# First layer's gate modulation on VectorE instead of TensorE, and two more PSUM banks in the second layer

## The chip, the core and the metric

The kernel runs on one NeuronCore of a Trainium2 chip, with float32 inputs and outputs. The metric is the device time of one execution in microseconds (us). TensorE, VectorE, ScalarE, GpSimd and SyncE are called by these names in the text, and PE, DVE, ACT, POOL and SP in the rows of the profile.

## What is computed

Three transformer layers follow each other on 256 tokens, the first also on 256 context tokens: a differential attention layer, a grouped attention layer, and a third with sparse attention, retention and a feed-forward part. The change concerns the modulation of the first two. Each layer multiplies silu(c) and silu(c_ctx) with a matrix `ada_w[i]` of 1024 x 3072. The first third of its product shifts the normed input, the second scales it and the last gates the layer's output.

```python
# first block, layer 0 (differential attention) and layer 1 (grouped attention), over x (256 tokens)
# and ctx (256 tokens), D = 1024
def adaln(cvec, w, b):
    m = jax.nn.silu(cvec) @ w + b
    return jnp.split(m, 3, axis=-1)
...
    for i in range(DEPTH):
        last = i == DEPTH - 1
        shift, scale, gate = adaln(c, ada_w[i], ada_b[i])
        shift, scale, gate = shift[:, None, :], scale[:, None, :], gate[:, None, :]
        cshift, cscale, cgate = adaln(c_ctx, ada_w[i], ada_b[i])
        h = rms_norm(x, pre_g[i]) * (1.0 + scale) + shift
        hc = rms_norm(xc, pre_g[i]) * (1.0 + cscale) + cshift
...
        x = x + gate * rms_norm(y, post_g[i])
        if not last:
            xc = xc + cgate * rms_norm(yc, post_g[i])
    return x
```

## The kernel before

**Products.** All weights stream from HBM in halves of 128 x 4 x 512 numbers (1 MB; "half 0" holds rows 0 to 511 of the matrix, "half 1" rows 512 to 1023) through six buffers `raw`, in the order of `loads_plan`. SyncE issues one load after the other, and load n waits until load n-6 has been used up. ScalarE rounds a half into one of three `w_hi` buffers (line 1372), VectorE writes the rest into `w_lo` (line 1951), and TensorE multiplies in three products for each block of 128 rows (lines 825 to 827). A unit (stage, c, t) is one column chunk c of 512 columns for one tile t of 128 tokens, 8 blocks and so 24 products.

**Modulation products.** `ada_half` (line 847) does without the split: four products of 32 rows each with `cstat`, straight from `raw`. `BESIDE_IN0` says beside which unit of the first layer's input stage `in0` such a pair of halves is worked off. Before the change the gate's two chunks ("ada0g", 0) and ("ada0g", 1) stand beside units (0, 3) and (1, 1), and the four chunks of the second layer's shift and scale ("ada1", 0 to 3) beside (2, 1), (3, 1), (4, 1) and (5, 0). ScalarE copies the product out of PSUM (`move`, line 1454). For shift and scale `mod_columns` (line 861) then turns the rows into columns, beside the units of `COLUMNS_IN0`, and VectorE adds the bias (`mod_sums`, line 2103). For the gate `gate_row` (line 871) multiplies the rows with `sel`, which spreads them to all partitions.

**The stage in0.** Units (0, 0) to (5, 3) run in this order on TensorE. Chunks 0 to 3 are queries and keys, and after unit n TensorE turns unit n-2 (line 922). ScalarE handles each unit in the order: copy of the turned unit n-2 (line 1505), then the copy of a modulation product of the unit before, then for chunks 4 and 5 the copy of the values. VectorE takes at tile 0 of chunk c the split of the half that comes third from the chunk's start. After unit (5, 2) TensorE computes the first two score blocks, then unit (5, 3), and then it waits for the first probabilities: 32 steps of attention (p = 0 to 31) with the units of chunks 6 and 7 between them. For them VectorE runs, in this order, `max0(0)`, `max0(1)` (line 2199), `comb0(0)`, `comb0(1)` (lines 2208 to 2214), the split of half 1 of chunk 6, and `max0(2)`. `comb0(p)` releases TensorE's turn of the probabilities (line 928). The exponentials between them are ScalarE's (line 1529).

**The stage in1.** Here the second layer's units (c, t) run. TensorE turns the context tiles' features in pairs of two blocks, `norm1c`, half of them after unit (2, 0), the other half after unit (2, 1) (`NORM_IN1`, line 885). A pair fills one PSUM bank, which VectorE frees once it has written the rests of both blocks (`lo1`, lines 2355 and 1986). Before the change pairs 0 and 1 use banks 4 and 5, and pairs 2 and 3 use them again. Unit (2, 2) is the first that reads these features, and it waits for the rest of each block. `GATE_IN1` places the second layer's gate rows after units (1, 0) and (2, 1), and VectorE finishes them in `gates1` (lines 2288 and 2291) in the unit after. When the units are done, TensorE waits until all turned blocks have been copied, and starts the second layer's scores.

## Times and profile before

| | us |
|---|---|
| three runs, median (lowest, highest) | 799.34 (798.61, 799.36) |
| the profiled execution | 799.71 |
| its span | 797.6 |

The profile shows one execution. The span is what lies between its first and last instruction, and 2.1 us of the execution's own time lie around it. A row of a timeline gives start, duration, engine, source line, operation, output and inputs, how many were merged into the row, and in brackets the idle time of the engine before it and what ended it.

### The profile page before, as it was taken

The numbers are of one execution on the slowest core, as the hardware profiler recorded it, in microseconds if no ns is written. First come the engines' busy times: TensorE is split into PE (matmuls) and PEld (weight loads), VectorE is DVE, ScalarE is ACT, GpSimd is POOL, SyncE is SP. The second block draws the span as 40 slices with busy tenths as digits, with TensorE's granted clock in tenths as the row PEclk, the third lists the DMA queues.
The fourth block names the chain that finished last, engine by engine and source line by source line (L and its number), as shares of the span: only waits on it lengthen the run. The fifth ranks groups of instructions, "written<-read, shape, count | busy, mean of one in ns | idle before, by whom it ended". The sixth has DMA issues, their size and how long they took to land.

```text
span 797.6 us, 11013 instructions
## 1 busy us (share of the span) xinstructions
PE 786.0 (99%) x4108; PEld 625.5 (78%) x4108; DVE 503.7 (63%) x873; ACT 394.0 (49%) x728; POOL 42.9 (5%) x55
## 2 busy tenths in 40 slices
PE   8999999999999999999999999999999999999998
PEld 5577787778777777777778887887788888888886
DVE  3475445225767875779856678799887645455454
ACT  3541313235878773575647646735345433443431
POOL 0120000000001001101100001300000000000000
PEclk9999999999999999999999999999999999999999
DMA  9974542464100046338333026983216665566521
GB/s 337 387 243 159 211 161 83 178 211 160 52 1 1 1 151 246 106 106 310 139 106 106 2 65 211 334 298 106 80 54 211 211 202 167 161 210 210 181 84 53
DMA packets 71303, 125.56 MB, mean 157 GB/s; under 512 B 2714, under 2 KB 28652, under 8 KB 71124
## 3 DMA queue, kind: packets, MB, share of 16 engines
q1 hardware_dynamic: 70208, 122.47, 44.2%
q0 software_dynamic: 512, 1.18, 0.6%
q10 hardware_dynamic: 532, 1.21, 0.4%
q8 instruction: 33, 0.54, 0.3%
q14 instruction: 18, 0.15, 0.1%
HBM read 123.79 MB, written 1.06 MB: 157 GB/s over the span
## 4 chain that ended last, share of the span: by engine, by line
PE 86%; DVE 6%; ACT 3%; DMA 2%; issue 1%; POOL 1%; SPq 1%; DVEq 0%; ACTq 0%
PE psum L825 20%; PE psum L827 19%; PE psum L826 19%; PE psum L1005 3%; PE psum L1335 3%; PE psum L928 3%; PE psum L1333 3%; PE psum L1334 3%; PE psum L1034 2%; PE psum L847 2%; DMA act_lo_as_f<-in_ada_w 2%; PE psum L1107 2%; DVE w_lo L1951 2%; PE psum L922 1%; PE psum L914 1%
## 5 line engine op out<-in xcount | busy, mean ns | idle before, releaser
L826 PE MATMUL psum<-w_lo,act_hi 128*128 128x512 f32 (+1 forms) x752 | 291.8, 388 | 0.0
L825 PE MATMUL psum<-w_hi,act_hi 128*128 128x512 f32 (+1 forms) x712 | 289.5, 407 | 1.2 <-DVE act_lo L2355 0.7
L827 PE MATMUL psum<-w_hi,act_lo 128*128 128x512 f32 (+1 forms) x712 | 276.9, 389 | 0.0
L1951 DVE TENSOR_TENSOR w_lo<-raw,w_hi 128x2048 fp32r<-128x2048 f32 (+1 forms) x70 | 157.9, 2263 | 104.9 <-ACT w_hi L1372 104.8
L1372 ACT ACTIVATE w_hi<-raw 128x2048 fp32r<-128x2048 f32 (+1 forms) x74 | 140.1, 1897 | 72.4 <-PE psum L827 36.9
L825 PEld LDWEIGHTS psum<-w_hi,act_hi 128*128 128x128 f32 x712 | 133.7, 188 | 43.6 <-issue 17.6
L826 PEld LDWEIGHTS psum<-w_lo,act_hi 128*128 128x128 f32 x752 | 141.6, 188 | 25.3 <-issue 1.0
L827 PEld LDWEIGHTS psum<-w_hi,act_lo 128*128 128x128 f32 x712 | 133.6, 188 | 28.6
L1919 POOL TENSOR_TENSOR rstd<-ms,half_neg 128x1 f32<-128x1 f32 (+3 forms) x38 | 36.3, 957 | 551.4 <-DVE ms L1992 551.4
L1529 ACT ACTIVATE sc<-psum,nmax 128x512 f32<-128x512 f32 (+1 forms) x64 | 36.9, 589 | 20.5 <-DVE nmax L2199 20.5
L1454 ACT ACTIVATE sc<-psum 128x512 f32<-128x512 f32 (+1 forms) x62 | 32.6, 527 | 15.3 <-PE psum L928 8.5
L2199 DVE TENSOR_REDUCE nmax<-psum 128x2 f32<-128x1024 f32 (+1 forms) x32 | 30.5, 954 | 10.3 <-PE psum L1005 10.2
L1334 PE MATMUL psum<-w_lo,act_hi 128*128 128x512 f32 x88 | 34.2, 389 | 0.0
L1875 ACT ACTIVATE sc<-psum 128x256 f32<-128x256 f32 x22 | 8.5, 385 | 50.5 <-PE psum L827 50.5
L1333 PE MATMUL psum<-w_hi,act_hi 128*128 128x512 f32 x80 | 31.2, 390 | 0.0
L1335 PE MATMUL psum<-w_hi,act_lo 128*128 128x512 f32 x80 | 31.1, 389 | 0.0
L928 PE MATMUL psum<-ident,sc 128*128 128x128 f32 x184 | 29.6, 274 | 1.0 <-ACT sc L1830 0.9
L1034 PEld LDWEIGHTS psum<-vbuf,sc 128*128 128x128 f32 x192 | 26.2, 191 | 3.6 <-ACT sc L1454 1.0
L1034 PE MATMUL psum<-vbuf,sc 128*128 128x128 f32 x192 | 26.7, 275 | 0.4 <-ACT sc L1454 0.4
L2785 DVE SCALAR_TENSOR_TENSOR sc<-sc,psum 128x256 f32<-128x256 f32 x22 | 9.2, 419 | 23.9 <-ACT sc L1875 23.9
L928 PEld LDWEIGHTS psum<-ident,sc 128*128 128x128 f32 x184 | 21.7, 142 | 2.5 <-ACT sc L1830 1.7
L1505 ACT ACTIVATE round_k<-psum 128x512 fp32r<-128x512 f32 x8 | 4.8, 599 | 33.6 <-PE psum L922 33.6
(272 smaller groups left out, 991.2 us busy)
## 6 DMA issues: line engine op xcount, KB each, us to landing
raw<-in_a_w_in SPq DMA_DIRECT2D x16, 1024.0 KB, 9.6
raw<-in_ada_w SPq DMA_DIRECT2D x16, 1024.0 KB, 5.3
raw<-in_w_out SPq DMA_DIRECT2D x12, 1024.0 KB, 5.2
raw<-in_w_gate SPq DMA_DIRECT2D x22, 512.0 KB, 4.2
raw<-in_w_up SPq DMA_DIRECT2D x22, 512.0 KB, 5.2
raw<-in_w_down SPq DMA_DIRECT2D x11, 1024.0 KB, 4.9
raw<-in_b_w_in SPq DMA_DIRECT2D x10, 1024.0 KB, 7.3
raw<-in_w_in SPq DMA_DIRECT2D x10, 1024.0 KB, 6.0
```

The costliest lines, as they stand in the source:

```text
L825: pe.matmul(oh, x_hi, hi, start=(k == 0), stop=False)
L826: pe.matmul(o[:, 0:n], x_hi, lo, start=False, stop=False)
L827: mm = pe.matmul(oh, x_lo, hi, start=False, stop=(k == KT - 1))
L928: mm = pe.transpose(o[:, tile_cols(i)], src[:, tile_cols(i)], ident[:])
L1034: mm = pe.matmul(o[:, 0:P], probs[:, tile_cols(i)], vbuf[:, NT - blocks + i, tile_cols(h)], start=(i == 0), stop=(i == blocks - 1))
L1333: pe.matmul(oh, x_hi, hi, start=(j == 0 and i == 0), stop=False)
L1334: pe.matmul(o, x_hi, lo, start=False, stop=False)
L1335: mm = pe.matmul(oh, x_lo, hi, start=False, stop=(last and i == 1))
L1372: ins = act.activation(hi, weights, ACTF.Copy)
L1529: seq.freed(act.activation(sc[:, 2 * (p % 2) + s, 0:n], psum[:, b, 0:n], ACTF.Exp, bias=nmax[:, p % 2, s:s + 1], accum_out=rsum[:, p % 2, ...
L1919: seq.note(pool.tensor_tensor(rstd[:, n:n + w], ms[:, n:n + w], half_neg[:, 0:w], ALU.pow).then_inc(s_powout, 1), s_powout)
L1951: ins = dve.tensor_tensor(rest, weights, hi.bitcast(F32), ALU.subtract)
```

## The change

The gate's product of the first layer is no longer taken on TensorE. VectorE multiplies each block of weight rows with one column of silu(c) or silu(c_ctx), a number per partition, and adds eight such blocks up in `gate0`. The sum over the partitions, which is left then, is done by the product that spread the rows before: its first operand is now a matrix of ones. These are 32 instructions of 128 x 512, half of them beside the units of chunk 4 (`SUMMED_IN0`), half beside those of chunk 5. The loads of the gate's weights come after chunks 4 and 5, and those of ("ada1", 0 to 3) move up to the places after chunks 0 to 3. The gain `post_g[0]` is loaded later, by SyncE's queue into `kT` in place of GpSimd's into `gate0`. In the second layer the four pairs of `norm1c` get the banks 4, 5, 6 and 7, and the second gate row stands after unit (2, 2).

```diff
@@ -54,15 +54,17 @@
 ADA0_ORDER = [0, 2, 1, 3]
 
 
-BESIDE_IN0 = {(0, 3): ("ada0g", 0), (1, 1): ("ada0g", 1)}
-BESIDE_IN0.update({(2 + c, 1 if c < 3 else 0): ("ada1", c) for c in range(4)})
-
-
-COLUMNS_IN0 = {(2 + c, 3 if c < 3 else 2): c for c in range(4)}
+BESIDE_IN0 = {(c, 1 if c else 3): ("ada1", c) for c in range(4)}
+
+
+COLUMNS_IN0 = {(c if c else 1, 3 if c else 0): c for c in range(4)}
+
+
+SUMMED_IN0 = {4: 0, 5: 1}
 
 
 BESIDE_IN1 = {(0, 0): 4, (1, 1): 5}
-GATE_IN1 = {(1, 0): 0, (2, 1): 1}
+GATE_IN1 = {(1, 0): 0, (2, 2): 1}
 
 
 NORM_IN1 = {(2, 0): range(0, 4), (2, 1): range(4, 8)}
@@ -79,6 +81,8 @@
         for t in range(NT):
             if (c, t) in BESIDE_IN0:
                 plan += both(*BESIDE_IN0[(c, t)])
+        if c in SUMMED_IN0:
+            plan += both("ada0g", SUMMED_IN0[c])
     for stage, chunks in (("out0", 2), ("in1", 5), ("out1", 2), ("in2", 6), ("out2", 2)):
         for c in range(chunks):
             plan += both(stage, c)
@@ -221,14 +225,17 @@
         put(("out0", 1, XT + t), 6 + t)
     norm("norm1")
     units("in1", range(3))
-    for pair in range(HALF_KT):
-        put(("norm1c", pair), 4 + pair % 2)
-    for c in range(3):
+    for c in range(2):
         for t in gemm_tiles("in1", c):
             put(("turn1", c, t), 2 + t)
     for c in range(2):
         put(("ada1", 4 + c, 0), 6 + c)
-        put(("gate1", 0, c), 6 + c)
+    put(("gate1", 0, 0), 6)
+    for pair in range(HALF_KT):
+        put(("norm1c", pair), 4 + pair)
+    for t in gemm_tiles("in1", 2):
+        put(("turn1", 2, t), 2 + t)
+    put(("gate1", 0, 1), 7)
     for p in range(XT * HEADS):
         put(("s1", p), 2 + p % 2)
         put(("t1", p), 6)
@@ -438,14 +446,19 @@
         s_idle, s_xturned = sem("idle_operands_ready"), sem("x_turned")
         s_hi0, s_f0, s_lo0 = sem("first_hi_ready"), sem("first_x_modulated"), sem("first_lo_ready")
         s_res, s_yret = sem("residual_ready"), sem("retention_head_done")
-        N_CIN, N_VEC, N_LATE = 3, 4, 10
-
-        mrow0g = gate0[:, 0, :]
+        s_sumused, s_summed, s_ones = sem("summed_half_used"), sem("gate_sum_ready"), sem("ones_ready")
+        N_CIN, N_VEC, N_LATE = 3, 4, 9
+
+        mrow1g = gate0[:, 0, :]
+
+
+        def gate_sum(s, c):
+            return gate0[:, s, c * COLS:(c + 1) * COLS]
 
         def mod_rows(l, c):
             if l == 0:
                 return mrow[:, c * COLS:(c + 1) * COLS]
-            return sc[:, 5 + c % 2, :] if c < HALF_KT else mrow0g[:, (c - 4) * COLS:(c - 3) * COLS]
+            return sc[:, 5 + c % 2, :] if c < HALF_KT else mrow1g[:, (c - 4) * COLS:(c - 3) * COLS]
 
         k_flat = kT[:].rearrange("p h n -> p (h n)")
         gain2, gain3 = gate0[:, 1, :], q_flat[:, D:2 * D]
@@ -566,7 +579,9 @@
 
         emptied, firsts = {}, 0
         for n, (stage, c, h) in enumerate(loads):
-            if not stage.startswith("ada"):
+            if stage == "ada0g":
+                emptied[n] = (s_sumused, 2 * c + h + 1)
+            elif not stage.startswith("ada"):
                 emptied[n] = released[half_no[(stage, c, h)]]
             elif h == 0:
                 firsts += 1
@@ -648,6 +663,7 @@
                     load(k_flat[:, 0:D], a["ada_b"][0, 2 * D:3 * D].partition_broadcast(P), s_par1)
                     load(k_flat[:, D:2 * D], a["ada_b"][1, 2 * D:3 * D].partition_broadcast(P), s_par1)
                     load(k_flat[:, 2 * D:3 * D], a["post_g"][1].partition_broadcast(P), s_par1)
+                    load(k_flat[:, 3 * D:4 * D], a["post_g"][0].partition_broadcast(P), s_par1)
                 if loads[n] == ("out1", 0, 0):
 
                     sp.wait_ge(s_res, NT)
@@ -864,12 +880,16 @@
 
             def gate_row(l, s, c):
 
-                rows = mod_rows(1, 4 + c) if l else mrow0g[:, c * COLS:(c + 1) * COLS]
-                pe.wait_ge(*moved(("ada1", 4 + c, 0) if l else ("ada0g", c, 0)))
+                if l:
+                    pe.wait_ge(*moved(("ada1", 4 + c, 0)))
+                    pick, rows = sel[:, s, :], mod_rows(1, 4 + c)
+                else:
+                    pe.wait_ge(s_ones, 1)
+                    pe.wait_ge(s_summed, 2 * c + s + 1)
+                    pick, rows = ones[:], gate_sum(s, c)
                 name = (f"gate{l}", s, c)
                 o = begin(name)
-                pe.matmul(o, sel[:, s, :], rows,
-                          start=True, stop=True).then_inc(bank_full(name), 1)
+                pe.matmul(o, pick, rows, start=True, stop=True).then_inc(bank_full(name), 1)
 
             def norm(stage, ks=range(KT)):
                 tiles = norm_tiles[stage]
@@ -1511,10 +1531,7 @@
                 before = (c, t - 1) if t else (c - 1, NT - 1)
                 if before in BESIDE_IN0:
                     stage, part = BESIDE_IN0[before]
-                    if stage == "ada0g":
-                        move(mrow0g[:, part * COLS:(part + 1) * COLS], (stage, part, 0))
-                    else:
-                        move(mod_rows(1, part), (stage, part, 0), wait_for=("mod1", part - 2) if part >= 2 else None)
+                    move(mod_rows(1, part), (stage, part, 0), wait_for=("mod1", part - 2) if part >= 2 else None)
                 if c in (4, 5):
                     move(vbuf[:, t, (c - 4) * COLS:(c - 3) * COLS], ("in0", c, t))
 
@@ -1908,6 +1925,7 @@
             seq = Sequence(moved)
             seq.note(pool.memset(half_neg[:], -0.5).then_inc(s_g, 1), s_g)
             pool.memset(zero[:], 0.0).then_inc(s_half, 1)
+            pool.memset(ones[:], 1.0).then_inc(s_ones, 1)
             pool.wait_ge(s_half, 1)
             n_pows = [0]
 
@@ -1925,7 +1943,6 @@
             pool.dma_start(rope_a[:], a["k_rope_a"]).then_inc(s_par, 16)
             pool.wait_ge(s_mod, 2)
             for dst, src in ((lamb[:], a["a_lambda"][0].partition_broadcast(P)),
-                             (gate0[:, 1, :], a["post_g"][0].partition_broadcast(P)),
                              (rope_b[:], a["k_rope_b"]), (rope_c[:], a["k_rope_c"]),
                              (qk_g[:], a["b_qk_g"][0].partition_broadcast(P)),
                              (qkn2[:, 0, :], a["q_norm_w_2"][0].partition_broadcast(P)),
@@ -2172,10 +2189,32 @@
                 if (c, t) in COLUMNS_IN0:
                     mod_sums(1, COLUMNS_IN0[(c, t)])
 
+            def gate_block(c, s, k):
+
+
+                n = load_no[("ada0g", c, k // HALF_KT)]
+                if k % HALF_KT == 0 and not s:
+                    dve.wait_ge(landed[n % RAW], landed_at[n])
+                w, value, total = raw_view(n)[:, k % HALF_KT, :], cols[:, 8 * s + k:8 * s + k + 1], gate_sum(s, c)
+                dve.wait_ge(*seq.last)
+                if k:
+                    ins = dve.scalar_tensor_tensor(out=total, in0=w, scalar=value, in1=total, op0=ALU.mult, op1=ALU.add)
+                else:
+                    ins = dve.tensor_scalar(total, w, value, None, ALU.mult)
+                done = s_summed if k == KT - 1 else s_v
+                seq.note(ins.then_inc(done, 1), done)
+
             def unit_in0(c, t):
                 unit0(c, t)
                 if t == 0:
                     split_through(half_no[("in0", c, 0)] + 2)
+                if c in SUMMED_IN0:
+                    for k in (2 * t, 2 * t + 1):
+                        for s in range(2):
+                            gate_block(SUMMED_IN0[c], s, k)
+                    if t % 2:
+                        dve.wait_ge(*seq.last)
+                        seq.note(dve.memset(ss[0:1, 255:256], 0.0).then_inc(s_sumused, 1), s_sumused)
 
             for c in range(5):
                 run_chunk("in0", c, unit_in0, ahead=3)
@@ -2278,7 +2317,7 @@
             sub_mean(3)
             gated(3)
             to_feature("turn_o0", [1, 3])
-            dve.wait_ge(s_par1, 48)
+            dve.wait_ge(s_par1, 64)
 
             def gates1(c):
 
@@ -2302,7 +2341,8 @@
                                                 ALU.add).then_inc(bank_free(nm), 1), nm)
                 for s in range(2):
                     dve.wait_ge(*seq.last)
-                    seq.note(dve.tensor_tensor(gate0[:, s, r], sc[:, 2 * c + s, :], gate0[:, 1, r], ALU.mult).then_inc(s_v, 1), s_v)
+                    seq.note(dve.tensor_tensor(gate0[:, s, r], sc[:, 2 * c + s, :], k_flat[:, 3 * D + c * COLS:3 * D + (c + 1) * COLS],
+                                               ALU.mult).then_inc(s_v, 1), s_v)
 
             def post_scale(l, t):
                 gate = gate1 if l else gate0[:, t // XT, :]
```

TensorE's order at the start of chunk 1, from the end of unit (1, 0) on; `sel` with `sc` is `mod_columns`, `ident` with `sc` the turn of unit (0, 2). Before:

```order
L827 MATMUL psum<-w_hi,act_lo 128x512
L922 MATMUL psum<-ident,sc 128x128 [waits bank4_free,rot_ready]
L922 MATMUL psum<-ident,sc 128x128 x3
L825 MATMUL psum<-w_hi,act_hi 128x512 [waits w_lo_ready,bank1_free]
L826 MATMUL psum<-w_lo,act_hi 128x512
L827 MATMUL psum<-w_hi,act_lo 128x512
```

Now, with `mod_columns` of ("ada1", 0) right behind the turn; it waits for bank 6, which ScalarE's copy of that product frees:

```order
L843 MATMUL psum<-w_hi,act_lo 128x512
L942 MATMUL psum<-ident,sc 128x128 [waits bank4_free,rot_ready]
L942 MATMUL psum<-ident,sc 128x128 x3
L877 MATMUL psum<-sel,sc 128x2 [waits bank7_free,bank6_free]
L877 MATMUL psum<-sel,sc 128x2 x3
L841 MATMUL psum<-w_hi,act_hi 128x512 [waits w_lo_ready,bank1_free]
L842 MATMUL psum<-w_lo,act_hi 128x512
L843 MATMUL psum<-w_hi,act_lo 128x512
```

The four turns and the four column products follow each other directly; before, the unit (1, 1) came first.

VectorE's order from the end of chunk 4 to the first maximum of the attention. Before (line 1951 is the split, 2103 and 2108 `mod_sums`, 2199 the maximum):

```order
L1951 TENSOR_TENSOR w_lo<-raw,w_hi 128x2048
L2103 TENSOR_TENSOR mod<-psum,cols 128x8
L2108 SCALAR_TENSOR_TENSOR mod<-mod,cols 128x8
L2185 TENSOR_TENSOR sc<-lamb 128x128
L2187 TENSOR_REDUCE lam_s<-sc 128x2
L1951 TENSOR_TENSOR w_lo<-raw,w_hi 128x2048
L2103 TENSOR_TENSOR mod<-psum,cols 128x8
L2108 SCALAR_TENSOR_TENSOR mod<-mod,cols 128x8
L2191 TENSOR_SCALAR lam_s<-lam_s 128x1
L2247 TENSOR_TENSOR qkn<-qkn 128x64
L2199 TENSOR_REDUCE nmax<-psum 128x2 x2
```

Now (1968 is the split, 2201 and 2203 the new sums, 2238 the maximum):

```order
L2217 MEMSET ss 1x1
L2224 TENSOR_TENSOR sc<-lamb 128x128
L2226 TENSOR_REDUCE lam_s<-sc 128x2
L1968 TENSOR_TENSOR w_lo<-raw,w_hi 128x2048
L2203 TENSOR_SCALAR gate<-raw,cols 128x512 x2
L2201 SCALAR_TENSOR_TENSOR gate<-raw,cols,gate 128x512 x6
L2217 MEMSET ss 1x1
L2201 SCALAR_TENSOR_TENSOR gate<-raw,cols,gate 128x512 x8
L2217 MEMSET ss 1x1
L2230 TENSOR_SCALAR lam_s<-lam_s 128x1
L2286 TENSOR_TENSOR qkn<-qkn 128x64
L2238 TENSOR_REDUCE nmax<-psum 128x2 x2
```

Behind the split of chunk 6's first half now stand 16 instructions on `gate0` and two that report, all ahead of the first maximum.

TensorE's order between units (2, 1) and (2, 2) of the second layer; `ident` with `zbuf` are the context's features, `gate` with `sel` the gate row. Before:

```order
L922 MATMUL psum<-ident,sc 128x128 [waits bank3_free,rot_ready]
L922 MATMUL psum<-ident,sc 128x128 x3
L885 MATMUL psum<-ident,zbuf 128x128 [waits bank4_free,xn1_ready]
L885 MATMUL psum<-ident,zbuf 128x128 x3
L885 MATMUL psum<-ident,zbuf 128x128 [waits bank5_free]
L885 MATMUL psum<-ident,zbuf 128x128 x3
L871 MATMUL psum<-gate,sel 128x512 [waits bank7_free]
L825 MATMUL psum<-w_hi,act_hi 128x512 [waits act_ready,w_lo_ready,bank0_free]
L826 MATMUL psum<-w_lo,act_hi 128x512
```

Now:

```order
L942 MATMUL psum<-ident,sc 128x128 [waits bank3_free,rot_ready]
L942 MATMUL psum<-ident,sc 128x128 x3
L905 MATMUL psum<-ident,zbuf 128x128 [waits bank6_free,xn1_ready]
L905 MATMUL psum<-ident,zbuf 128x128 x3
L905 MATMUL psum<-ident,zbuf 128x128 [waits bank7_free]
L905 MATMUL psum<-ident,zbuf 128x128 x3
L841 MATMUL psum<-w_hi,act_hi 128x512 [waits act_ready,w_lo_ready,bank0_free]
L842 MATMUL psum<-w_lo,act_hi 128x512
```

The features no longer wait for banks 4 and 5, and the gate row is no longer ahead of unit (2, 2). It stands behind it and the next turn:

```order
L843 MATMUL psum<-w_hi,act_lo 128x512
L942 MATMUL psum<-ident,sc 128x128 [waits bank2_free,rot_ready]
L942 MATMUL psum<-ident,sc 128x128
L892 MATMUL psum<-gate,sel 128x512 [waits bank7_free]
L841 MATMUL psum<-w_hi,act_hi 128x512 [waits w_lo_ready,bank1_free]
L842 MATMUL psum<-w_lo,act_hi 128x512
```

## Rows read from the trace of the kernel before

**Rows 1.** The page: busy time and share of the span, granted clock in 40 slices.
```profile
PE 786.0 (99%) x4108; PEld 625.5 (78%) x4108; DVE 503.7 (63%) x873; ACT 394.0 (49%) x728; POOL 42.9 (5%) x55
...
PEclk9999999999999999999999999999999999999999
...
GB/s 337 387 243 159 211 161 83 178 211 160 52 1 1 1 151 246 106 106 310 139 106 106 2 65 211 334 298 106 80 54 211 211 202 167 161 210 210 181 84 53
```
**Rows 2.** The chain that ended last, in order of time: start, length, what.
```profile
59.21 1.85 PE psum L847 x16
...
184.34 0.79 PE psum L861 x8
...
311.20 1.72 PE psum L871 x4
```
**Rows 3.** Timeline of TensorE behind unit (1, 0) and the turn of unit (0, 2).
```profile
66.93 0.47 PE L825 MATMUL psum<-w_hi,act_hi 128*128 128x512 f32 x1
```
**Rows 4.** Timeline of ScalarE, the copy of ("ada0g", 0).
```profile
67.71 0.59 ACT L1454 ACTIVATE gate<-psum 128x512 f32<-128x512 f32 x1
```
**Rows 5.** Timeline of SyncE's queue, two pairs of loads at chunk 4's end.
```profile
162.25 3.09 SPq L616 DMA_DIRECT2D raw<-in_ada_w  x2
165.38 27.07 SPq L616 DMA_DIRECT2D raw<-in_a_w_in  x4
```
**Rows 6.** Timeline of ScalarE, rounding of chunk 6's half 0.
```profile
174.16 1.92 ACT L1372 ACTIVATE w_hi<-raw 128x2048 fp32r<-128x2048 f32 x1 [2.19 <-DMA raw<-in_a_w_in]
```
**Rows 7.** Timeline of VectorE from that half's split to the first probabilities.
```profile
176.11 2.29 DVE L1951 TENSOR_TENSOR w_lo<-raw,w_hi 128x2048 fp32r<-128x2048 f32 x1 [8.75 <-ACT w_hi L1372]
185.16 0.17 DVE L2103 TENSOR_TENSOR mod<-psum,cols 128x8 f32<-128x8 f32 x1 [6.76 <-PE psum L861]
...
186.16 1.82 DVE L2199 TENSOR_REDUCE nmax<-psum 128x2 f32<-128x1024 f32 x2 [0.38 <-PE psum L1005]
...
189.48 0.75 DVE L2214 SCALAR_TENSOR_TENSOR sc<-sc,rinv 128x512 f32<-128x512 f32 x1
...
197.18 0.75 DVE L2214 SCALAR_TENSOR_TENSOR sc<-sc,rinv 128x512 f32<-128x512 f32 x1
```
**Rows 8.** Timeline of TensorE, the turns of steps 0 and 2.
```profile
191.90 0.60 PE L928 MATMUL psum<-ident,sc 128*128 128x128 f32 x4
...
198.50 0.60 PE L928 MATMUL psum<-ident,sc 128*128 128x128 f32 x4
```
**Rows 9.** Groups of VectorE's instructions by form: busy, mean ns | idle before.
```profile
L2214 DVE SCALAR_TENSOR_TENSOR sc<-sc,rinv 128x512 f32<-128x512 f32 x16 | 12.0, 752 | 0.6
...
L2009 DVE TENSOR_SCALAR zbuf<-xs,rstd 128x1024 f32<-128x1024 f32 x4 | 3.0, 750 | 0.9 <-POOL rstd L1919 0.9
```
**Rows 10.** Timeline of VectorE in out0, pairs without and with a wait.
```profile
313.07 1.28 DVE L2301 TENSOR_TENSOR sc<-psum,kT 128x512 f32<-128x512 f32 x2
314.39 1.42 DVE L2305 TENSOR_TENSOR gate<-sc,gate 128x512 f32<-128x512 f32 x2
```
**Rows 11.** Timeline of TensorE between units (2, 1) and (2, 2) of in1.
```profile
390.97 1.41 PE L885 MATMUL psum<-ident,zbuf 128*128 128x128 f32 x8 [1.03 <-DVE ss L1986]
392.21 1.02 PE L871 MATMUL psum<-gate,sel 128*128 128x512 f32 x2
...
396.70 0.47 PE L825 MATMUL psum<-w_hi,act_hi 128*128 128x512 f32 x1 [0.70 <-DVE act_lo L2355]
```
**Rows 12.** Timeline of VectorE, rests of pair 2, `gates1`, last turned copy.
```profile
396.13 0.76 DVE L2355 TENSOR_TENSOR act_lo<-vbuf,act_hi 128x256 fp32r<-128x256 f32 x2
...
402.88 0.69 DVE L2288 TENSOR_TENSOR kT<-psum,kT 128x512 f32<-128x512 f32 x1
...
410.17 0.42 DVE L2393 SCALAR_TENSOR_TENSOR round_v<-psum,round_k 128x256 fp32r<-128x256 f32 x1 [0.29 <-ACT round_k L1663]
```
**Rows 13.** Timeline of TensorE, the second layer's first scores.
```profile
410.95 0.39 PE L1097 MATMUL psum<-round_k,round_q 128*128 128x512 f32 x1
```
**Rows 14.** Waits of TensorE, the longest: line, releaser, us in total, times, longest us.
```profile
PE psum L936 <- DVE w_hi L2073: 1.5, 1, 1.5
```

1 line of the change is left out of this document (added).

## The prediction

> **What bounds the kernel now.** Read first the page's busy times. TensorE works 786.0 of the span's 797.6 us, at full clock in all 40 slices [rows 1], so time comes only out of TensorE's own instructions and its few waits. Read next the chain that ended last: on it stand the gate's products, the column products and the gate rows [rows 2]. What leaves TensorE's queue there is gained in full. What makes TensorE wait is lost in full. Last, read the timelines of TensorE and of the engine it meets at the three places where the order differs: the start of chunk 1 [rows 3, 4], the start of the attention [rows 5 to 8] and the second layer's context features [rows 11 to 13]. Each term below is made there, as a change of the moment at which TensorE passes.
>
> **A. The gate's products go: -3.70.** A pair of halves is 16 instructions of `ada_half`, 1.85 us on the chain [rows 2], and two pairs go. The four pairs of ("ada1", c) only change places. The columns (8 in 0.79 us) and the gate rows (four in two rows of 1.72 us, so 0.86 for two) keep their number, with `ones` in place of `sel` for layer 0. Small edges around the removed pairs, under 0.2 us each, are left out.
>
> **B. Columns too close behind their product: +1.37.** `mod_columns` of ("ada1", 0) now stands right behind the turn of unit (0, 2). TensorE gets there where unit (1, 1) starts today, 66.93 [rows 3]. It needs ScalarE's copy of the product, and ScalarE copies the turned unit first, then the product. The copy in that place today, of ("ada0g", 0), ends at 67.71 + 0.59 = 68.30 [rows 4]. TensorE has nothing else in its queue, so 68.30 - 66.93 = 1.37 us are lost. The other three sets of columns stand two units, over 10 us, behind their product and wait for nothing.
>
> **C. The start of the attention: +5.75.** VectorE now has 16 sums, `gate_block` for the second gate chunk, between the split of chunk 6's half 0 and the first maximum. Before, it sat idle there for 6.76 us behind the split [rows 7], and that is the cover. I walk through it.
> - When the half is rounded. Today SyncE has four loads of `in0` in a row behind a pair of `ada1` [rows 5], and the rounding starts at 174.16, ended by the load [rows 6]. The whole stretch shifts by B, by two sets of columns done earlier (2 x 0.79) and by one pair of gate products fewer (1.85): 1.37 + 1.58 - 1.85 = +1.10, so 175.26. The loads ahead of it are the second gate pair now, and the load behind the second waits for a sum, some 4 us later than its place today, so fewer transfers run beside it. Bounds: nothing gained, or three loads of 1.05 MB at the best slice's 387 GB/s [rows 1], 2.7 us each from 162.25 on, so 170.4, which is 3.8 earlier. I take 1.0 earlier, 174.3, nearer to the row as it stands.
> - The split's end lies 4.24 behind the rounding's start (176.11 + 2.29 - 174.16) [rows 6, 7]: 178.5.
> - The sums. The instruction of the same form, operands and shape is L2214, 752 ns [rows 9]. Each sum waits for the one before, since it adds to it or follows it in `seq`. What a wait does to the spacing: the two instructions of L2301 without one are 1.28 long together, those of L2305 with one 1.42 [rows 10]. One such instruction lasts 0.69 [rows 12], so the spacing is 0.59 without and 0.73 with, or 0.04 more than the duration. A sum costs 0.75 + 0.04 = 0.79. The two first ones of a chunk are TENSOR_SCALAR, of which 1024 columns take 750 ns [rows 9]: between 0.37 and 0.75, I take 0.5 and the 0.04. With two small reports of 0.1: 14 x 0.79 + 2 x 0.54 + 0.2 = 12.3, to 190.8. Bounds: 16 at a spacing of 0.60, 9.6, or 16 at 0.85, 13.6.
> - The small instructions of lambda and q norm take 0.4 and the first maximum starts at 191.25. From it to the end of the first probabilities are 189.48 + 0.75 - 186.16 = 4.07 us of VectorE and ScalarE in turn [rows 7]: 195.3.
> - TensorE would be at the turn of step 0 at 191.90 [rows 8] - 3.70 + 1.37 = 189.57. It stands there 195.3 - 189.57 = **5.75 us**. Today it does not wait, since the probabilities are ready at 190.23. Behind it are the score blocks of step 2 and all units of chunk 6, so nothing can go ahead of it.
>
> The same sums in chunk 4 cost nothing: VectorE idles 8.75 us before the split at 176.11 [rows 7], so 12.3 us of sums spread over four units fit beside it, and split (5, 1) is reached at about the time when `w_hi` is there. They need TensorE only at the gate rows near 311 [rows 2].
>
> The Trainium skill, page "VectorE: DVE Perf Modes", section "The DRAIN you can't avoid", says that a semaphore after each VectorE instruction costs nothing beside the pipeline's own drain. By that the sums would be spaced at about 0.66 and C would be some 2.1 us less. The pair with the wait is 0.14 longer [rows 10], so this trace speaks against it, and my sum stays as it is.
>
> **D. The second step: +1.1.** Behind `comb0(0)` VectorE runs `comb0(1)`, the split of half 1 and `max0(2)` before `comb0(2)`. The two are 197.18 - 189.48 = 7.70 us apart [rows 7]. TensorE's turns of steps 0 and 2 are 198.50 - 191.90 = 6.60 apart [rows 8]. Once TensorE runs behind VectorE there, it waits 7.70 - 6.60 = 1.1 again. Bounds 0 (the maximum needs scores that TensorE will have done earlier, a wait of 1.02 us) and 1.5. Later steps have slack.
>
> **E. The second layer's context features: +1.46.**
> - The four banks take away a wait of 1.03 for VectorE's rest L1986 between the pairs [rows 11]. But unit (2, 2) needs those same rests: it waits for L2355, until 396.70, behind a rest that VectorE writes at 396.13 [rows 11, 12]. VectorE has no idle time ahead of that row, so TensorE gets to the same wait earlier and leaves it at the same time: gain 0. Bound: -1.73 (1.03 + 0.70), if VectorE was itself held back by the banks.
> - The gate row (two products, 0.86 by [rows 2]) stood in that hole and now stands behind it: +0.86.
> - `gates1` of the second chunk (two of 0.69 [rows 12], about 1.33 together) now runs a unit later, ahead of the last turned rests, which end at 410.17 + 0.42 = 410.59 [rows 12]. The wait of 0.29 there goes: 410.59 + 0.86 + 1.33 - 0.29 = 412.5, against TensorE's first scores at 410.95 + 0.86 = 411.81 [rows 13]: about +0.6. Bounds 0 and 1.3.
>
> **Nothing** is charged for the memset of `ones` (POOL works 42.9 us in all [rows 1]), for `post_g` on SyncE's queue (its reader is at 313.07 [rows 10], 20 us behind its load, and if it were late VectorE would pass it on to TensorE one for one), or for ("ada1", c) being loaded earlier: the bytes up to chunk 4 are the same. The sums read `raw` for longer than four products do, and buffers freed late could hold up half (6, 1), which is used 15 us later.
>
> **The sum.** -3.70 + 1.37 + 5.75 + 1.1 + 0.86 + 0.6 = +5.98. The profiled execution took 799.71, so 805.7. The median of the runs is 0.37 lower, so **805.3 us**. With the bounds of the sums (2.7 less, 1.3 more), of the rounding (2.8 less, 1.0 more), of D and of E taken two at a time, the case reaches from 801.5 to 808.0.
>
> **The rivals.**
> 1. *TensorE's clock falls in the stall.* The clock is granted in full in every slice [rows 1], but the longest wait of this trace is 1.5 us, at its very start [rows 14], so no row says what 5.75 us of idleness do. If the clock went to 1.2 GHz, each us of work behind the stall would take two until it rose. With 2 us of work so, it is +2: 807.3. For it: the stall is four times the longest seen. Against: the sums could be shorter. Chance 0.2. (The Trainium skill, "TensorE: Matmul & The Clock Gate", Part 1 "The HAM clock gate", says that an idle TensorE is set back to 1.2 GHz and raised again by activity. No row here shows it.)
> 2. *The banks do gain.* VectorE's chain before 396 was held by the two banks: E is then -1.73 without the 0.86, 3.2 lower with the rest as forecast: 802.1. Chance 0.12.
> 3. *The sums are hidden.* C and D vanish if TensorE finds the probabilities ready: they may be late by nothing from 189.57 on, so the maximum must start by 185.5, and 16 sums from 178.5 take under 6.6 us, 0.4 each. That is half of every row of 512 columns of this form. An early load (174.3 - 2.8) helps, but then they still may take only 9.4 us. Time: -3.70 + 1.37 + 0.86 + 0.6 = -0.87: 798.5, no change. Chance 0.09.
> 4. *Hidden, and the banks gain:* the change does what it is written for. -0.87 - 3.2 = -4.1: 795.3, faster. Chance 0.04. Only this one ends on the other side.
>
> **How the numbers follow.** The forecast case has 0.55, and rivals 1 to 4 have 0.20, 0.12, 0.09 and 0.04. The range 801.0 to 808.5 holds the forecast case, the second rival and the first at its price; it leaves out the last two and the tail of a longer fall of the clock. A measurement of this kernel can tell about 0.2%, or 1.6 us, from no change: 797.7 to 800.9. Faster is the fourth rival and a part of the third, 0.06. Same is the rest of the third with the lowest end of the second, 0.10. Slower is 0.84.
>
> **What would show each step.** In the profile of the changed kernel: TensorE's row of `mod_columns` in chunk 1 with some 1.4 us idle behind ScalarE's copy (B). Behind the split at 178 sixteen rows of `gate<-raw` of about 0.75 us without gaps, and before the turn of the first probabilities some 5.7 us of idle TensorE released by VectorE (C), before the next turn about 1 (D). Between units (2, 1) and (2, 2) no wait for L1986, and one of about 2.6 us for the rest in place of the 0.70 (E). A digit under 9 in the clock's row would show rival 1. The prediction is wrong if the sums take under 0.6 us each, if the split of chunk 6 ends before 176, or if VectorE shows idle time between the rests before unit (2, 2).

## The result, and the profile after

The changed kernel takes **808.3 us** (median of four runs, 806.61 to 809.3), the kernel before 799.25 us (four runs, 798.61 to 799.36). The ratio is 1.0113, with a 95% interval of 1.0093 to 1.0133: slower by 9.05 us. The forecast was slower, 805.3 us with a range of 801.0 to 808.5. The range holds the time, near its upper end. The likeliest case was 3 us short.

The page of the profiled execution (807.59 us, span 805.6) has the same busy time of TensorE as [rows 1], and one slice in which the granted clock is no longer full:

```profile
PE 786.0 (98%) x4076; PEld 627.8 (78%) x4076; DVE 526.4 (65%) x909; ACT 391.7 (49%) x726; POOL 42.5 (5%) x55
...
PEclk9999999998999999999999999999999999999999
```

That the busy time stayed is the first thing to stumble over, since 32 products went, 3.7 us by [rows 2]. Products at half clock are busy for longer, and that filled the gap: in e11 below, with the same products at full clock, TensorE is busy for 781.9 us. TensorE's waits (line, releaser, us in total, times, longest) show three that [rows 14] and the rest of that view did not have, L948, L877 and L1117, and one that grew from 0.70 to 2.69, L841:

```profile
PE psum L948 <- DVE sc L2253: 5.7, 1, 5.7
PE psum L841 <- DVE act_lo L2395: 2.7, 1, 2.7
PE psum L956 <- DVE w_hi L2090: 1.5, 1, 1.5
PE psum L877 <- ACT sc L1474: 1.2, 1, 1.2
...
PE psum L1117 <- DVE round_v L2433: 0.7, 1, 0.7
```

VectorE's timeline from the split of chunk 6's half 0 to the first probabilities, beside [rows 7]:

```profile
175.62 2.29 DVE L1968 TENSOR_TENSOR w_lo<-raw,w_hi 128x2048 fp32r<-128x2048 f32 x1 [4.49 <-ACT w_hi L1392]
178.02 1.01 DVE L2203 TENSOR_SCALAR gate<-raw,cols 128x512 f32<-128x512 f32 x2
179.06 4.69 DVE L2201 SCALAR_TENSOR_TENSOR gate<-raw,cols,gate 128x512 f32<-128x512 f32 x6
...
183.97 6.26 DVE L2201 SCALAR_TENSOR_TENSOR gate<-raw,cols,gate 128x512 f32<-128x512 f32 x8
...
190.53 1.81 DVE L2238 TENSOR_REDUCE nmax<-psum 128x2 f32<-128x1024 f32 x2
...
193.84 0.75 DVE L2253 SCALAR_TENSOR_TENSOR sc<-sc,rinv 128x512 f32<-128x512 f32 x1
```

The sums run without a gap for 12.2 us, and the idle time of 6.76 us of [rows 7] is gone. For step 2 VectorE in its turn waits for TensorE's scores:

```profile
201.46 0.69 DVE L2238 TENSOR_REDUCE nmax<-psum 128x2 f32<-128x512 f32 x1 [2.06 <-PE psum L1025]
```

TensorE at the columns of chunk 1, beside [rows 3]:

```profile
66.17 0.60 PE L942 MATMUL psum<-ident,sc 128*128 128x128 f32 x4
67.94 1.05 PE L877 MATMUL psum<-sel,sc 128*128 128x2 f32 x8 [1.18 <-ACT sc L1474]
```

The columns start 1.77 us behind the start of the turn. Before, unit (1, 1) started 0.35 behind it (66.58 and 66.93), so the delay is 1.42 us. It is larger than the idle time in brackets, because that is counted from the end of a product, and the next one can start before this end (products of 0.39 us start 0.23 apart).

TensorE's timeline at the start of the attention, beside [rows 8]:

```profile
188.58 0.39 PE L843 MATMUL psum<-w_hi,act_lo 128*128 128x512 f32 x1
194.65 1.11 PE L948 MATMUL psum<-ident,sc 128*128 128x128 f32 x4 [5.68 <-DVE sc L2253]
195.69 0.79 PE L1025 MATMUL psum<-round_k,round_q 64*128 64x512 f32 x2
...
203.87 0.60 PE L948 MATMUL psum<-ident,sc 128*128 128x128 f32 x4
```

After 5.68 us of idleness the four turns last 1.11 us, where they last 0.60 in [rows 8]. Stretches of 2 us (length, busy time of PE, PEld, DVE, ACT and POOL with instruction counts, then the granted clock, then DMA share and GB/s) say why:

```profile
192.00:194.00 2.00, 0.00 (x0) 0.00 (x0) 0.94 (x4) 2.00 (x8) 0.00 (x0) 0.88 1.03 394
194.00:196.00 2.00, 1.35 (x6) 1.02 (x8) 1.45 (x5) 2.00 (x4) 0.00 (x0) 0.50 1.05 400
196.00:198.00 2.00, 2.00 (x8) 1.16 (x7) 2.00 (x1) 0.91 (x2) 0.00 (x0) 0.50 1.04 390
198.00:200.00 2.00, 2.00 (x10) 1.81 (x9) 1.40 (x2) 0.57 (x1) 0.00 (x0) 0.50 0.56 203
200.00:202.00 2.00, 2.00 (x14) 1.61 (x14) 0.54 (x1) 1.87 (x8) 0.00 (x0) 0.91 0.00 0
```

The clock was at 0.50, the level of 1.2 GHz, when TensorE resumed, and stayed there until about 200.4, for 5.7 us of its work. In the second layer, TensorE's timeline in unit (2, 2) and at the first scores, beside [rows 11, 13]:

```profile
401.30 0.47 PE L841 MATMUL psum<-w_hi,act_hi 128*128 128x512 f32 x1 [2.69 <-DVE act_lo L2395]
401.60 0.50 PE L842 MATMUL psum<-w_lo,act_hi 128*128 128x512 f32 x1
401.90 0.63 PE L843 MATMUL psum<-w_hi,act_lo 128*128 128x512 f32 x1
...
405.93 1.02 PE L892 MATMUL psum<-gate,sel 128*128 128x512 f32 x2
...
418.84 0.47 PE L1117 MATMUL psum<-round_k,round_q 128*128 128x512 f32 x1 [0.67 <-DVE round_v L2433]
```

The wait for L1986 is gone, the wait for the rest is 2.69 instead of 0.70, and behind it a product of 0.39 takes 0.63, so the clock fell here too. Read as moments of TensorE, the whole difference is this:

| TensorE at | before | after | shift |
|---|---|---|---|
| start of the last product of unit (5, 3) | 191.67 | 188.58 | -3.09 |
| turn of step 0 | 191.90 | 194.65 | +2.75 |
| turn of step 2 | 198.50 | 203.87 | +5.37 |
| gate rows of the first layer | 311.04 | 316.05 | +5.01 |
| turn ahead of the context's features, in1 | 389.34 | 394.38 | +5.04 |
| first scores of the second layer | 410.95 | 418.84 | +7.89 |
| span | 797.6 | 805.6 | +8.0 |

Up to the attention the change does gain. It loses 5.8 us at step 0, 2.6 between steps 0 and 2, and 2.9 in in1, and gains another 0.4 between step 2 and the gate rows.

### The profile page after: what moved, and what is told of

It is laid out like the page before. It is cut to its first block, busy times and chain, and to the rows that moved or that the text cites. A ratio compares the mean times of both kernels' runs of the same rounds, so it can differ in the third digit from the quotient of the medians.

```text
span 805.6 us, 10986 instructions
## 1 busy us (share of the span) xinstructions
PE 786.0 (98%) x4076; PEld 627.8 (78%) x4076; DVE 526.4 (65%) x909; ACT 391.7 (49%) x726; POOL 42.5 (5%) x55
## 4 chain that ended last, share of the span: by engine, by line
PE 82%; DVE 9%; ACT 3%; DMA 3%; issue 1%; POOL 1%; SPq 1%; DVEq 0%; ACTq 0%
PE psum L841 19%; PE psum L843 18%; PE psum L842 18%; PE psum L1054 3%; PE psum L1025 3%; PE psum L948 3%; PE psum L1355 2%; PE psum L1353 2%; PE psum L1354 2%; DVE w_lo L1968 2%; DMA act_lo_as_f<-in_ada_w 2%; PE psum L1127 2%; PE psum L863 2%; DVE gate L2201 1%; PE psum L942 1%
## 5 line engine op out<-in xcount | busy, mean ns | idle before, releaser
L841 PE MATMUL psum<-w_hi,act_hi 128*128 128x512 f32 (+1 forms) x712 | 290.0, 407 | 3.2 <-DVE act_lo L2395 2.7
L841 PEld LDWEIGHTS psum<-w_hi,act_hi 128*128 128x128 f32 x712 | 134.4, 189 | 44.4 <-issue 18.2
L1474 ACT ACTIVATE sc<-psum 128x512 f32<-128x512 f32 (+1 forms) x62 | 32.5, 526 | 14.7 <-PE psum L948 8.7
L948 PE MATMUL psum<-ident,sc 128*128 128x128 f32 x184 | 30.1, 278 | 6.7 <-DVE sc L2253 5.7
L948 PEld LDWEIGHTS psum<-ident,sc 128*128 128x128 f32 x184 | 22.0, 144 | 8.5 <-DVE sc L2253 6.1
L1525 ACT ACTIVATE round_q<-psum 128x512 fp32r<-128x512 f32 x8 | 4.8, 598 | 35.7 <-PE psum L942 35.7
```

Of the source, the lines that this page charges most:

```text
L841: pe.matmul(oh, x_hi, hi, start=(k == 0), stop=False)
L948: mm = pe.transpose(o[:, tile_cols(i)], src[:, tile_cols(i)], ident[:])
```

## The experiments

The theory after the result had four parts: the gate's products are a true gain of about 4 us; VectorE's order makes the wait at step 0; TensorE's idleness pulls its own clock down, which is paid on top; and the second layer's part is a loss by itself. All runs below stand against the kernel before, run beside them, 798.8 to 798.9 us. The changed kernel was not run again beside them. Its 808.3 us belong to a kernel before of 799.25, so some 0.4 us of every difference from 808.3 can come from that alone.

**e1: the sums ahead of the split.**

```diff
-                if t == 0:
+                if t == 0 and c < 5:
                     split_through(half_no[("in0", c, 0)] + 2)
                 if c in SUMMED_IN0:
...
+                if (c, t) == (5, NT - 1):
+                    split_through(half_no[("in0", 5, 0)] + 2)
```

> The changed kernel with one move: VectorE takes the 16 sums of the second gate chunk before the split of chunk 6's half 0, not behind it. Theory (the stall is VectorE's order: it idles 4.5 us before that split, then 12.3 us of sums stand ahead of the first maximum): sums from about 171.2 to 183.5, split to 185.8, maximum at 186, first probabilities at about 190.1, against a TensorE that is there at 189.0. The wait of 5.7 us shrinks to about 1.1, the clock stays at 1.00 behind it, and steps 0 and 2 lie 7.7 apart instead of 9.2: 808.3 - 4.6 - 1.5 = 802.2. Rival (the wait is for the second gate pair's loads or the split itself is then late for unit (6, 0)): the sums end no earlier than 189 and the time stays above 806.

Measured: 802.14 us, ratio 1.0042 (1.0027 to 1.0057). VectorE, then TensorE:

```profile
179.14 6.26 DVE L2201 SCALAR_TENSOR_TENSOR gate<-raw,cols,gate 128x512 f32<-128x512 f32 x8
185.45 2.29 DVE L1968 TENSOR_TENSOR w_lo<-raw,w_hi 128x2048 fp32r<-128x2048 f32 x1
```
```profile
192.03 0.66 PE L948 MATMUL psum<-ident,sc 128*128 128x128 f32 x4 [1.11 <-DVE sc L2255]
```

The same instructions, one of them moved, are worth 6.2 us (5.8 if both kernels are taken against their own kernel before). The wait is 1.11 us and the clock behind it is 1.00. So the order was at fault, not the number of sums, nor the loads. Steps 0 and 2 lie 7.92 apart. The wait between them stands at the product with the values of step 1, not at the turn of step 2, and it is for ScalarE's copy of the turned probabilities (L1474), which stands behind exponentials that wait for VectorE's maximum:

```profile
196.82 0.69 ACT L1546 ACTIVATE sc<-psum,nmax 128x512 f32<-128x512 f32 x1 [2.52 <-DVE nmax L2240]
```
```profile
199.40 0.71 PE L1054 MATMUL psum<-vbuf,sc 128*128 128x128 f32 x4 [0.66 <-ACT sc L1474]
199.95 0.60 PE L948 MATMUL psum<-ident,sc 128*128 128x128 f32 x4
```

**e2: unused products in the wait.**

```diff
+                if p == 0:
+                    o = begin(("t0", 0))
+                    for _ in range(22):
+                        pe.matmul(o, round_q[:, 0, 0:P], round_k[:, 0, :], start=True, stop=True)
                 pe.wait_ge(s_comb, p + 1)
```

> The changed kernel with 22 products of 128x512 (0.227 us each, 5.0 us), whose result nobody reads, ahead of TensorE's first turn of probabilities, where it stood idle for 5.7 us at full clock and then worked at 0.50 for 5.5 us. It separates the wait from the clock. Theory (the fall of the clock is the idleness's doing and is paid on top of the wait): the turn of step 0 stays at the same time, the clock stays 1.00 behind it, steps 0 and 2 lie 7.7 apart (VectorE's distance) instead of 9.2: 808.3 - 1.5 = 806.8. Rival (the low clock comes from elsewhere, or what it costs is hidden by VectorE's steps): 808.3, no change.

Measured: 806.86 us, ratio 1.0094 (1.0079 to 1.0109), 1.4 under the changed kernel; steps 0 and 2 7.92 apart. As the theory has it, but the spread of these runs (804.95 to 807.11) is as large as the effect. e9 and e10 repeat it with nothing else disturbed.

**e3: the second layer's part undone**, and **e4: the columns a unit later.**

```diff
-GATE_IN1 = {(1, 0): 0, (2, 2): 1}
+GATE_IN1 = {(1, 0): 0, (2, 1): 1}
...
-        put(("norm1c", pair), 4 + pair)
+        put(("norm1c", pair), 4 + pair % 2)
```

> The changed kernel with the second layer's part undone: pairs of the context's features in banks 4, 5, 4, 5 and the second gate row between units (2, 1) and (2, 2). From the turn ahead of unit (2, 2) to the first scores TensorE needed 24.46 us after the change and 21.61 before. Theory (gate row out of the hole, one wait of 2.7 us that pulls the clock down to 0.50 for some 3.5 us, and gates1 ahead of the last turned rest): all of the 2.85 comes back, 805.4. Rival (my forecast's terms alone, the gate row's 0.86 and the rest's 0.6, with the clock's fall there by chance): 806.8. Second rival (the four banks gain something that the clock's fall hides): 806.8 or more.

Measured: 804.59 us, ratio 1.0067 (1.0052 to 1.0082): 3.7 back, 0.8 more than expected, and closer to the theory than to my forecast's 1.5. The expectation took the kernel before as its measure. From the first turn of the context's features to the first scores TensorE needs 27.40 us in e3 and 30.83 in the changed kernel, 3.43 more, but 27.96 in the kernel before. e3 has the banks and the gate row of the kernel before, so these last 0.6 come from elsewhere. e8 finds the larger part of them.

```diff
-BESIDE_IN0 = {(c, 1 if c else 3): ("ada1", c) for c in range(4)}
+BESIDE_IN0 = {(0, 3): ("ada1", 0), (1, 2): ("ada1", 1), (2, 1): ("ada1", 2), (3, 1): ("ada1", 3)}
-COLUMNS_IN0 = {(c if c else 1, 3 if c else 0): c for c in range(4)}
+COLUMNS_IN0 = {(1, 1): 0, (2, 0): 1, (2, 3): 2, (3, 3): 3}
```

> The changed kernel with the columns of (ada1, 0) one unit later, after unit (1, 1), and with the product of (ada1, 1) one unit later too, after (1, 2), its columns after (2, 0), since the banks are given out in that order. Nothing else moves. Theory: the wait of 1.18 us for ScalarE's copy goes and everything behind it starts earlier, but the stall before the first probabilities is set by VectorE behind the half's load, so part of the gain is given back there: between 807.1 (all kept, if the load moves with it) and 808.3 (all given back, if the load's landing sets the stall's end). Rival (another copy is late in its place): a wait of its own at the later columns, 808.3.

Measured: 805.6 us, ratio 1.0086 (1.007 to 1.0103): 2.7 back, where the wait is 1.2 and the delay 1.4. This expectation was wrong, and it led to a find. In the changed kernel's own profile the wait of 1.18 us at the columns left the clock alone. e1 and e2 have the same program up to there, and theirs shows this (e1, stretches as above):

```profile
68.00:70.00 2.00, 1.72 (x12) 1.58 (x13) 1.51 (x5) 2.00 (x2) 0.00 (x0) 1.00 0.43 157
70.00:72.00 2.00, 2.00 (x7) 1.53 (x6) 1.93 (x1) 0.03 (x1) 0.00 (x0) 0.65 0.00 0
72.00:74.00 2.00, 2.00 (x6) 1.60 (x5) 0.36 (x1) 0.00 (x0) 0.00 (x0) 0.50 0.00 0
74.00:76.00 2.00, 2.00 (x10) 1.63 (x10) 0.00 (x0) 0.00 (x0) 0.00 (x0) 1.00 0.00 0
```

The stretch is all products at full load and costs 1.7 us more than its twin in the changed kernel's profile. So the small wait costs 1.4 in some executions and 3.1 in others. The runs of e2 fit this: three took 806.85 to 807.11 at a mean clock of 0.997, and the fourth 804.95 at 1.00. So does the median of e4 (1.4 and most of 1.7). That this is the whole of e4's excess is not shown, since the fall in in1 also comes and goes, and so does a part of the cost at step 0: in e4's profile steps 0 and 2 lie 8.14 apart, 1.08 less than in the changed kernel's, because there the clock fell 3.4 us before TensorE's wait was over and was full again at 197.

**e5: all three waits designed out.** To e3's banks this adds:

```diff
-SUMMED_IN0 = {4: 0, 5: 1}
+SUMMED_IN0 = {3: 0, 4: 1}
...
+BESIDE_IN0 = {(0, 3): ("ada1", 0), (1, 2): ("ada1", 1), (2, 1): ("ada1", 2), (5, 0): ("ada1", 3)}
+COLUMNS_IN0 = {(1, 1): 0, (2, 0): 1, (2, 3): 2, (5, 2): 3}
```

> The changed kernel with its gain kept and its three waits designed out: sums beside chunks 3 and 4 instead of 4 and 5, so that VectorE has none between the split of chunk 6's first half and the first maximum; ada1's products beside (0, 3), (1, 2), (2, 1) and (5, 0), its columns two units behind each (after (1, 1), (2, 0), (2, 3) and (5, 2)); banks and gate row of the second layer as before. Theory (the gate's products are worth 3.7 us, and all else that the change cost came from these three waits and the falls of the clock behind them): 798.9 - 3.7 = 795.2, clock at 1.00 throughout. Rival (VectorE's sums in chunk 3 delay the rotated units or the rests, or the six loads of a chunk come late): a new wait in chunk 3 or 4 and more than 797.

Measured: 795.73 us, ratio 0.9961 (0.9949 to 0.9974), faster than before, clock 1.00 throughout. The theory's 795.2 was close. The rival's wait is there, once, but not its time of over 797. TensorE in unit (4, 0), and VectorE ahead of it:

```profile
142.72 0.50 PE L838 MATMUL psum<-w_hi,act_hi 128*128 128x512 f32 x1 [1.27 <-DVE w_lo L1965]
```
```profile
137.35 3.12 DVE L2198 SCALAR_TENSOR_TENSOR gate<-raw,cols,gate 128x512 f32<-128x512 f32 x4
140.38 2.28 DVE L1965 TENSOR_TENSOR w_lo<-raw,w_hi 128x2048 fp32r<-128x2048 f32 x1
```

**e6: e1, e3 and e4 together.**

> e1 (sums ahead of the split, in chunks 4 and 5) with the columns later as in e4 and the second layer as in e3. Theory: the gate's products gone, -3.7; left of the costs are the wait of 1.1 before the first probabilities and the 1.3 by which steps 0 and 2 are then farther apart: 798.9 - 3.7 + 1.1 + 1.3 = 797.6. The clock stays at 1.00, since a wait of 1.1 at that place did not lower it in e1. Rival (costs overlap, the single gains do not add up): above 799.

Measured: 796.9 us, ratio 0.9974 (0.9964 to 0.9984), 0.7 under the expectation. The parts add up, the costs at least: the wait at step 0 is 1.11 us again, steps 0 and 2 lie 7.92 apart again, and the clock is at 1.00.

**e7: the second layer's part alone, on the kernel before**, and **e8: one bank more, the gate row left in its hole.**

> The kernel before with the second layer's part of the change alone: four banks for the context's pairs, second gate row after unit (2, 2). Theory (the banks' wait only moves to unit (2, 2), which waits for VectorE's rests; the gate row loses its hole, +0.86; the last turned rest is late, +0.7; and a single wait of 2.4 to 2.7 us lowers the clock in part of the runs, 1.7 lost): between 798.9 + 1.5 = 800.4 and 802.1. Rival (the four banks gain 1.0 to 1.7 by themselves): 798.9 or less.

Measured: 802.18 us, ratio 1.004 (1.0028 to 1.0053), 3.4 slower. One of the five runs took 800.39 at a mean clock of 0.999, the other four 802.14 to 803.04 at 0.996 to 0.998, as the theory has it for a run without and with the fall. TensorE in unit (2, 2) of e7:

```profile
395.98 0.47 PE L828 MATMUL psum<-w_hi,act_hi 128*128 128x512 f32 x1 [2.80 <-DVE act_lo L2358]
```

```diff
-        put(("norm1c", pair), 4 + pair % 2)
+        put(("norm1c", pair), (4, 5, 6, 4)[pair])
```

> The kernel before with pair 2 of the context's features in bank 6 (pairs in banks 4, 5, 6, 4) and the gate row where it was, between units (2, 1) and (2, 2): more banks without the gate row's move. Theory (VectorE writes the rests without a pause, so an earlier turn brings them no earlier, and the wait of 1.0 moves to unit (2, 2)): 798.9, within 0.3. Rival (banks are worth it when the gate row stays): 798.2 to 797.9.

Measured: 798.97 us, ratio 1.0001 (0.9993 to 1.001). TensorE in e8:

```profile
390.44 0.66 PE L888 MATMUL psum<-ident,zbuf 128*128 128x128 f32 x4 [0.21 <-DVE ss L1989]
390.93 1.02 PE L874 MATMUL psum<-gate,sel 128*128 128x512 f32 x2
...
396.25 0.47 PE L828 MATMUL psum<-w_hi,act_hi 128*128 128x512 f32 x1 [1.53 <-DVE act_lo L2358]
```

One wait shrinks from 1.03 to 0.21 and the next grows from 0.70 to 1.53: 1.73 before, 1.74 here. VectorE sets the moment, and banks move only where TensorE stands idle. From the split ahead of them (384.08 before) to the rests that unit (2, 2) waits for (396.13) VectorE takes 12.05 us before and in e7, 12.04 in e8. The theory's reason, that it writes the rests without a pause, is not right, though: it pauses on the way, by the profile for GpSimd's `rstd`. Before, and in the changed kernel:

```profile
394.21 0.61 DVE L2427 SCALAR_TENSOR_TENSOR sc<-psum,rstd,qk_g 128x128 f32<-128x128 f32 x2 [1.22 <-POOL rstd L1919]
```
```profile
398.81 0.61 DVE L2467 SCALAR_TENSOR_TENSOR sc<-psum,rstd,qk_g 128x128 f32<-128x128 f32 x2 [0.86 <-POOL rstd L1937]
```

The pause is 1.22 in all three kernels that keep the gate's products on TensorE (before, e7, e8) and 0.86 or 0.87 in all ten that sum on VectorE, with the banks moved or not. So this gain of 0.36 us belongs to the first layer's part of the change. Its cause was not found. What costs in e7 is the gate row out of its hole (0.86 from start to start), the late `gates1` (0.84 with the wait of 0.69 at the first scores), and that one wait of 2.80 lowers the clock (1.6), where two of 1.03 and 0.70 with work between do not: 3.3 together.

**e9 and e10: the wait at step 0 alone, idle and filled.** e9 is e3 with e4, e10 the same with e2's products.

> The changed kernel with the columns later (e4) and the second layer as before (e3), so that of the three waits only the one before the first probabilities is left, about 6 us. Theory: -3.7 for the gate's products, +5.9 for the wait, and 1.3 plus 1.3 by which steps 0 and 2 are farther apart (VectorE's distance, and what of the clock's 3.4 us lies beyond it): 798.8 + 4.8 = 803.6, with the clock at 0.50 for 7 us in every run. Rival (the falls of the clock are at random places and not tied to the waits): falls in chunk 1 or in1 as before, and a spread of over 2 us.

> e9 with the 22 unused products of e2 in the wait. The probabilities are as late as before, only TensorE is not idle. Theory: clock 1.00 throughout, steps 0 and 2 lie 7.9 apart as in e1 and e2 and not 9.2, and nothing else changes: 1.3 below e9, 802.3. Rival (the clock's fall is hidden by VectorE's steps in the end): same as e9.

Measured: e9 802.74 us, ratio 1.005 (1.0037 to 1.0063), its five runs within 1.1 us (802.55 to 803.6) and each with a mean clock of 0.995 or 0.996. e10 801.64 us, ratio 1.0033 (1.0021 to 1.0045), its six runs from 801.28 to 802.12, all at 1.00. The two do not overlap. Both lie under their expectations, by 0.9 and 0.7. TensorE in e9, then in e10:

```profile
193.37 1.11 PE L945 MATMUL psum<-ident,sc 128*128 128x128 f32 x4 [5.80 <-DVE sc L2250]
...
202.88 0.60 PE L945 MATMUL psum<-ident,sc 128*128 128x128 f32 x4
```
```profile
187.88 5.15 PE L1060 MATMUL psum<-round_k,round_q 128*128 128x512 f32 x22
193.80 0.66 PE L945 MATMUL psum<-ident,sc 128*128 128x128 f32 x4 [0.77 <-DVE sc L2255]
...
201.72 0.60 PE L945 MATMUL psum<-ident,sc 128*128 128x128 f32 x4
```

22 products that nobody reads make the kernel 1.1 us faster, because TensorE's clock is full when the probabilities arrive. Steps 0 and 2 are 9.51 apart in e9 and 7.92 in e10. The clock was at 0.50 from about 192.9 to 199.75 in e9, and TensorE at work for 6.4 us of it, which takes 3.2 us from it. Yet only 1.6 of them are above the 7.92 of a full clock. The rival of random falls is out for this wait: by its mean clock e9's fall is in every run, and its profile has no other until its last microsecond.

**e11: e5 with one split ahead of four sums.**

```diff
+                if (c, t) == (3, 2):
+                    split_through(half_no[("in0", c, 0)] + 3)
                 if c in SUMMED_IN0:
```

> e5 with one split moved: in chunk 3 VectorE takes the split of chunk 4's half 1 ahead of tile 2's four sums. In e5 those sums end at 140.5, the split ran until 142.7 and TensorE waited 1.27 us for it, while its rounded half was there at 137.5. Theory: the wait goes, 795.7 - 1.3 = 794.4. Rival (the sums then delay the rotation of unit (3, 3) or the next rests, and TensorE waits there): 795.7.

Measured: **794.12 us**, ratio 0.9941 (0.9928 to 0.9953), the fastest kernel here and 14.2 us under the changed one, with the same sums on VectorE. Its page:

```profile
PE 781.9 (99%) x4076; PEld 625.1 (79%) x4076; DVE 526.3 (66%) x909; ACT 392.1 (50%) x726; POOL 42.2 (5%) x55
...
PEclk9999999999999999999999999999999999999999
```

## Why the prediction was right, and what it missed

| term | forecast | measured in the profile after, from start to start of TensorE's rows |
|---|---|---|
| A, products removed | -3.70 | -4.1 (4.08 between the turn of (0, 2) and step 0 in e11) |
| B, wait for ScalarE's copy | +1.37 | +1.42, and 1.7 more where the clock falls |
| C, wait at step 0 | +5.75 | +5.84 (5.68 idle) |
| D, steps 0 to 2 | +1.1 | +2.62; +1.32 at full clock (e1, e2, e6, e10) |
| E, in1 | +1.46 | +2.85: 3.29 of cost, 0.44 given back |
| elsewhere | 0 | -0.64 |

They add up to the +8.0 of the span. Of the last row, 0.41 lie ahead of the turn of (0, 2). They are chance, since TensorE gets to it at 65.97 to 66.66 in the kept profiles, whichever the kernel. Between step 2 and the gate rows are -0.36. There the kernels with sums on VectorE take 112.18 to 112.29 us and those without 112.45 to 112.54, so this is a small gain that the forecast lacked. Its cause is not shown.

**A** was too small by what I had set aside as edges, 0.2 for each pair. It is the one forecast gain, and e11 shows it undiluted. e11's 4.8 us under the kernel before are more than A. By its profile the rest lies in the gain just named and in VectorE's shorter pause in in1.

**B** was right in size. That so short a wait could lower the clock at all was not foreseen.

**C** came out step by step: rounding forecast at 174.3, measured 173.67; split's end 178.5 and 177.9; 16 sums in 12.3 and 12.2; maximum 191.25 and 190.53; probabilities 195.3 and 194.6. Each moment came 0.6 to 0.7 earlier, and TensorE too (the 0.41 and A's 0.4), so the wait kept its size. Eight sums in a row took 6.26 us, which is 0.75 and seven spacings of 0.787, where I had put 0.79. So the third and fourth rivals, which needed 0.4 a sum, never had a chance, though I had given them 0.13 together.

**D and the first rival.** What came is the first rival, not the case that I gave 0.55. I made the fall of the clock a rival with a chance of 0.2, though the forecast itself held a wait four times as long as any in [rows 14]. It then happened in every profile with that wait (after, e3, e4, e9). "Against: the sums could be shorter" was an argument about C, not about the clock. The Trainium skill, "TensorE: Matmul & The Clock Gate", Part 1 "The HAM clock gate", has an idle TensorE set back to 1.2 GHz, and the runs agree: 0.50 behind each wait of 5.7 us or more, and behind some of the shorter ones.

The path of D was wrong too. The forecast let TensorE wait for `comb0(2)`. In the changed kernel it does not wait between the two steps; VectorE waits 2.06 us for it, and the 2.62 are the clock's. At full clock it does wait, by e1 0.66 us at the product before, for ScalarE's copy. That +1.32 lies near the forecast's 1.1 is partly luck. The clock and D must not be added, either, since work at half clock fills the time in which TensorE would have waited. The four profiles with the long wait show it. In them the clock, counted over quarters of a microsecond, took 2.9, 2.6, 1.7 and 3.2 us of TensorE's work (after, e3, e4, e9). The steps lie 9.22, 8.99, 8.14 and 9.51 apart, each within 0.3 of the 6.60 before plus that loss, and never under the 7.92 of a full clock. So 0.2 to 1.6 us came through. The price of 2 us had no row behind its "2 us of work". That it came near the whole excess is luck: the clock cost 1.3 here and 1.6 in in1, where the rival had no fall at all.

**E** had the mechanism of the banks, and e7 and e8 show its claim that they gain nothing, against the second rival at 0.12. Its reason was misread: VectorE does have idle time ahead of the rests (1.22 us by the profile before), but for GpSimd and not for a bank. By the letter of the last sign, idle time of VectorE between the rests, the prediction would even be wrong, since the changed kernel has 0.86 us of it. The shorter pause is most of the 0.44 given back. The gate row (0.87, forecast 0.86) and the late `gates1` (0.83, forecast 0.6) were right too. Missing was again the clock. I had forecast one wait of 2.6 us in the place of two short ones and not asked what that does: 1.59 us between the wait's end and the next turn (405.71 - 401.30 = 4.41, before 399.52 - 396.70 = 2.82).

Against the forecast's +5.98 the profiled execution has 1.5 more in D, 1.4 in E and 0.1 in B and C, and less by 0.4 in A and 0.6 elsewhere. The range held the time because the first rival's price lay inside it. The median is 0.7 above the profiled execution. The two slowest runs, 809.01 and 809.3, have the lowest mean clocks, 0.991 and 0.989, which would fit one more fall such as e1's at the columns. No trace shows them.

## What to carry to other kernels

Work moved to an idle engine is hidden only if it stands behind nothing that the bound engine needs soon. Look at where in that engine's queue it lands, not at its share of busy time: the same 32 sums cost 5.8 us in one place and nothing in another (e11). Once a forecast holds a wait of TensorE longer than any in the trace, its clock is part of the forecast and no rival. What the clock takes is then set against the waits that TensorE would have had behind it, and only what is beyond them counts. And a hole that another wait makes is a good place for small work. Before taking work out of it, ask what will fill it.
